# Bias of the first units as one fp32 pass, two modulation pieces in an earlier loop, and norm steps inside the mixers' order

## The reference

```
for l in range(DEPTH):                      # DEPTH = 2
    ml = adaln_chunks(sc_lat @ w_mod[l] + b_mod[l])      # 9 vectors of 1024: shift, scale, gate, three times
    mc = adaln_chunks(sc_ctx @ w_mod[l] + b_mod[l])
    xl = xl + 0.5 * ml[2] * swiglu(modulate(rms_norm(xl, norm_ffn1[l]), ml[0], ml[1]), ffn1_w13[l], ffn1_w2[l])
    xc = ...                                             # the same for the context tokens
    h_ctx = modulate(rms_norm(xc, norm_mix[l]), mc[3], mc[4])
    h_lat = modulate(rms_norm(xl, norm_mix[l]), ml[3], ml[4])
    mix_c, mix_l = hybrid_mixer(h_ctx, h_lat, ...)       # w_in, attention A, attention B, Mamba-2 scan
    xl = xl + ml[5] * (mix_l @ w_out[l])
    xl = xl + 0.5 * ml[8] * swiglu(modulate(rms_norm(xl, norm_ffn2[l]), ml[6], ml[7]), ffn2_w13[l], ffn2_w2[l])
def modulate(h, shift, scale): return h * (1 + scale) + shift
```

## Time and profile before

| what | value |
|---|---|
| median of three runs | 1889.11 us (1888.89 to 1890.87) |
| profiled execution, its own time | 1888.78 us |
| its span | 1887.1 us |
| TensorE busy | 1811.9 us (96%) |
| VectorE busy | 1423.3 us (75%) |
| ScalarE busy | 752.0 us (40%) |
| HBM read | 252.60 MB |
| TensorE on the chain that ended last | 84% |

### The profile page before, as it was taken

The page is one execution under the profiler, slowest core; times in us unless marked ns, Lnnn a source line. Parts: engine busy times, 40 slices in busy tenths (PEclk is TensorE's granted clock), DMA queues, the critical chain, the costliest instruction groups (busy, mean ns, idle before and its releaser), DMA issues.

```text
span 1887.1 us, 26111 instructions
## 1 busy us (share of the span) xinstructions
PE 1811.9 (96%) x9314; PEld 1496.1 (79%) x9314; DVE 1423.3 (75%) x2351; ACT 752.0 (40%) x1147; POOL 51.6 (3%) x101
## 2 busy tenths in 40 slices
PE   8999999997999899899999999999999799899999
PEld 5788888886776577688888888888888578589999
DVE  5887877788877767887777678777786888756665
ACT  4322222246656656222222372222224654754342
POOL 1000000000000000000000000000000000000000
PEclk8899999998998899899999999999999899979999
DMA  8444444422312033534444423444440332134543
GB/s 352 179 151 183 147 159 168 182 80 93 119 45 90 1 134 116 197 133 178 155 156 161 151 75 148 159 168 162 156 156 29 114 111 88 48 112 178 180 178 110
DMA packets 37585, 259.47 MB, mean 137 GB/s; under 512 B 4369, under 2 KB 5841, under 8 KB 7441
## 3 DMA queue, kind: packets, MB, share of 16 engines
q1 hardware_dynamic: 26066, 182.32, 26.5%
q0 software_dynamic: 11456, 76.32, 11.0%
HBM read 252.60 MB, written 5.24 MB: 137 GB/s over the span
## 4 chain that ended last, share of the span: by engine, by line
PE 84%; DVE 6%; ACT 6%; issue 3%; DMA 1%; POOL 0%; ACTq 0%; DVEq 0%; POOLq 0%
PE ps L1514 25%; PE ps L1515 25%; PE ps L1516 25%; PE ps L1622 1%; DVE mod_prod L951 1%; ACT w_hi L546 1%; ACT n_t L598 1%; PE ps L1830 1%; DMA scale_w<-scale_in 1%; PE ps L1772 1%; PE ps L1891 1%; PE ps L1795 1%; DVE x_res L1056 1%; PE ps L1805 1%; PE ps L1645 1%
## 5 line engine op out<-in xcount | busy, mean ns | idle before, releaser
L1514 PE MATMUL ps<-h_hi,w_hi 128*128 128x512 f32 (+1 forms) x1840 | 680.3, 370 | 26.3 <-DVE w_lo L933 10.4
L1515 PE MATMUL ps<-h_lo,w_hi 128*128 128x512 f32 (+1 forms) x1840 | 673.7, 366 | 0.0
L1516 PE MATMUL ps<-h_hi,w_lo 128*128 128x512 f32 (+1 forms) x1840 | 672.9, 366 | 0.0
L1514 PEld LDWEIGHTS ps<-h_hi,w_hi 128*128 128x128 f32 x1840 | 350.5, 190 | 90.7 <-issue 22.9
L1516 PEld LDWEIGHTS ps<-h_hi,w_lo 128*128 128x128 f32 x1840 | 350.2, 190 | 57.4
L1515 PEld LDWEIGHTS ps<-h_lo,w_hi 128*128 128x128 f32 x1840 | 350.6, 191 | 56.6 <-issue 1.2
L928 DVE TENSOR_TENSOR w_lo<-raw,w_hi 128x2048 fp32r<-128x2048 f32 x132 | 301.9, 2287 | 82.3 <-ACT w_hi L546 82.2
L1056 DVE SCALAR_TENSOR_TENSOR x_res<-ps,abg,x_res 128x256 f32<-128x256 f32 x584 | 248.4, 477 | 151.2 <-PE ps L1516 150.2
L546 ACT ACTIVATE w_hi<-raw 128x2048 fp32r<-128x2048 f32 x132 | 252.2, 1911 | 268.0 <-PE ps L1516 268.0
L951 DVE CUSTOM_DVE_ANT_0 mod_prod<-mod_raw,cb 128x1024 f32<-128x1024 f32 x256 | 301.5, 1218 | 2.6 <-ACT cb L738 2.5
L1514 PE MATMUL ps<-a_hi,w_hi 128*128 128x512 f32 (+1 forms) x640 | 235.5, 368 | 16.1 <-DVE x_res L1056 12.5
(11 more groups left out here) (231 smaller groups left out, 1594.9 us busy)
## 6 DMA issues: line engine op xcount, KB each, us to landing
raw<-ffn_in SPq DMA_DIRECT2D x132, 1024.0 KB, 4.8
mod_raw<-mod_in POOLq DMA_DIRECT2D x68, 1024.0 KB, 5.0
raw<-proj_in SPq DMA_DIRECT2D x20, 1024.0 KB, 4.9
raw<-out_w_in SPq DMA_DIRECT2D x8, 1024.0 KB, 4.7
x_spill<-x_res SPq DMA_DIRECT2D x2, 2048.0 KB, 7.2
x_res<-x_spill SPq DMA_DIRECT2D x2, 2048.0 KB, 7.9
scale_w<-scale_in POOLq DMA_DIRECT2D x4, 512.0 KB, 13.1
x_res<-x_in SPq DMA_DIRECT2D x2, 1024.0 KB, 11.3
```

Source lines behind the costliest of these rows:

```text
L1514: pe.matmul(dst, w_hi[:, slot, wsl], hi, start=first, stop=False)
L1515: pe.matmul(dst, w_hi[:, slot, wsl], lo, start=False, stop=False)
L1516: return pe.matmul(dst, w_lo[:, slot, wsl], hi, start=False, stop=last)
```

## The change

- **Bias.** `unit_bias` multiplies the fp32 weights in `raw` with the fp32 shift in `abg`, 16 matmuls of two columns in place of 32 fp32r ones of four. It stands at the start of `first_unit`, which also waits until PSUM bank 4 has been read. `shift_r`, its split on VectorE and the reduction go. Because `raw` slot 0 is read later, SP waits for `bias_mm` ahead of the FFN's loop of loads and ahead of a mixer's load 2. With 256 tokens the mean moves from k = 2 to k = 5.
- **Modulation pieces 14 and 15** leave the start of FFN 1. FFN 0's turns 1 to 4 take six tiles each (pieces 4 to 9), turns 5 to 9 four (10 to 14), the last turn piece 15.
- **Norm steps in the order.** In a mixer n.0 to n.8, e.0 (`first_scaled`), dv.0 (`derive`), la.0 (the layer's small vectors) and S.-1 (the split of unit 2) are steps of `WEAVE`; before, they were done ahead of all others. R is in five parts, and both lists are new throughout.

```
-        MOD_PRE = {0: (2, 2), 1: (14, 2)}
-        STRETCH = {0: [(1, PAIRS - 1, 4)], 1: [(1, PAIRS - 1, 16)], ...
-        LAST_PIECE = {0: 13}
+        MOD_PRE = {0: (2, 2)}
+        STRETCH = {0: [(1, 5, 4), (5, PAIRS - 1, 10)], 1: [(1, PAIRS - 1, 16)], ...
+        LAST_PIECE = {0: 15}
...
-                "cv.0 E.0 E.1 S.0 T0.0 T.2 E.2 R.0 R.1 R.2 E.3 cv.1 T.3 T.4 cv.2 S.1 R.3 E.4 E.5 si.0 cv.3 S.2 si.1 si.2 si.3 "
+                "dv.0 n.0 n.1 n.2 n.3 T0.0 T.2 Ta.4 n.4 n.5 e.0 la.0 S.-1 E.0 E.1 Tb.4 Ta.5 n.6 n.7 Tb.5 n.8 cv.0 E.2 R.0 R.1 E.3 "
...
-                "cv.0 T0.0 cv.1 T.2 E.0 E.1 E.2 R.0 R.1 T.3 T.4 T.5 S.0 E.3 si.0 T.6 T.7 E.4 R.2 S.1 cv.2 cv.3 R.3 S.2 E.5 E.6 "
+                "dv.0 la.0 T0.0 n.0 n.1 n.2 T.2 n.3 n.4 n.5 Ta.4 n.6 n.7 Tb.4 e.0 Ta.5 Tb.5 n.8 S.-1 cv.0 cv.1 E.0 E.1 E.2 Ta.6 "
...
                     sp.dma_start(raw_of(1), ffn_in[f, 1]).then_inc(raw_in[1], 16)
+
+                    sp.wait_ge(bias_mm, NORM_OF_FFN[f])
...
+                    if m == 2:
+                        sp.wait_ge(bias_mm, 3 * layer + 1)
...
-            def split_shift(n):
...
-                dve.tensor_reduce(bias[:, :, :], ps[:, BIAS_AT, 0:8]...
+                dve.tensor_copy(bias[:, :, :], ps[:, BIAS_AT, 0:4].rearrange("p (m s) -> p m s", m=2)).then_inc(bias_done, 1)
...
-                if f == 1:
-                    mod_pieces(q0, cnt // 2)
                 split(0, f, 1)
...
+                if f == 1:
+                    dve.wait_ge(cb_ready, 6)
...
-                turn(i, None if q is None else i + (q - lo))
+                    if (f, lo) == (0, 1):
+                        with dve.Fori(0, 2) as t:
+                            a, b, c = (tiles_of(3 * t + (q + k)) for k in range(3))
+                            turn(2 * t + 1, a + b[:2])
+                            turn(2 * t + 2, b[2:] + c)
...
-            def unit_bias(n, slot):
-                pe.wait_ge(shift_done, 2 * n)
+            def unit_bias(n):
+                pe.wait_ge(derive_s, DERIVED_AB[n])
                 for m in range(2):
                     for k in range(KT):
-                        ...two matmuls, w_hi and w_lo by shift_r[:, k, :]
+                        last = pe.matmul(ps[:, BIAS_AT, 2 * m:2 * m + 2], raw[:, 0, 256 * k + P * m:256 * k + P * m + P],
+                                         abg[:, n, 1, :, k], start=(k == 0), stop=(k == KT - 1))
...
                 split_ready(0, turn)
+                pe.wait_ge(*evac)
+                unit_bias(n)
                 for k in range(KT):
...
-                    if k == 2:
+                    if k == (2 if nt == T else 5):
                         mean(n, nt)
-                    elif k == 5:
-                        unit_bias(n, 0)
```

More of the change, by code:

```diff
@@ L480, in load_stretches @@
                 for lo, hi, q0 in STRETCH[f]:
-                    if q0 is not None:
+                    if (f, lo) == (0, 1):
+                        with pool.Fori(0, 2) as t:
+                            for q in range(3):
+                                load_piece(3 * t + (q0 + q))
+                    elif q0 is not None:
                         with pool.Fori(lo, hi) as i:
@@ L693, in mixer @@
                     if kind == "E":
-                        if j >= 2:
+                        if j < 2:
+                            first_evacuation(layer, j)
+                        else:
                             evacuate(layer, j)
+                    elif kind == "n" and j < KT:
+                        norm_tile(3 * layer + 1, j, T, base)
                     elif kind == "S":
@@ L743, in first_evacuation @@
                 act.wait_ge(pads, layer + 1)
-                for j in range(2):
-                    act.wait_ge(scaled_s, 2 * n - 1 + j)
-                    for s in range(2):
-                        x = act.activation(xpad[:, j, s, 2:2 + LAT], ps[:, j, s * LAT:(s + 1) * LAT], ACT.Identity, bias=bias[:, j, s:s + 1])
-                    x.then_inc(pj_evac, 1)
+                act.wait_ge(scaled_s, 2 * n - 1 + j)
+                for s in range(2):
+                    x = act.activation(xpad[:, j, s, 2:2 + LAT], ps[:, j, s * LAT:(s + 1) * LAT], ACT.Identity, bias=bias[:, j, s:s + 1])
+                x.then_inc(pj_evac, 1)
             def evacuate(layer, g):
@@ L870, in decay_rows @@
                     act.activation(lam[0:16, 72:76], r[2].rearrange("p (c t) -> p c t", c=TT)[:, :, P - 1], ACT.Exp).then_inc(row_act, 1)
-                else:
+                elif part == 4:
                     act.wait_ge(row_act, ra + 8)
@@ L1020, in first_scaled, with norm_tile @@
                     tt(ps[:, m, 0:nt], ps[:, m, 0:nt], n_rstd[:, 0:nt], ALU.mult).then_inc(scaled_s, 1)
[L1022 to L1031 removed]
+            def norm_tile(n, d, nt):
+                if d == 0:
+                    dve.wait_ge(acc_done, 7 * n + 7)
+                    dve.wait_ge(rstd_done, 2 * n + 2)
+                if d < KT:
                     if d >= 2:
@@ L1034, in norm_rest @@
                     tt(n_t[:, d % 2, 0:nt], x_res[:, d, 0:nt], n_rstd[:, 0:nt], ALU.mult).then_inc(t_done, 1)
-                    if d >= 1:
-                        remainder(d - 1)
+                if d >= 1:
+                    dve.wait_ge(h_hi_s, 8 * n + d)
+                    tt(h_lo[:, d - 1, 0:nt], n_t[:, (d - 1) % 2, 0:nt], h_hi[:, d - 1, 0:nt], ALU.subtract).then_inc(h_lo_s, 1)
+            def norm_rest(n, nt, after={}):
+                for d in range(KT + 1):
+                    norm_tile(n, d, nt)
                     if d in after:
                         after[d]()
-                remainder(KT - 1)
             def product(f, i, nt, hi, lo):
@@ L1087, in ffn_phase, with down @@
                 derive(n, "g")
-                def down(i, units, add_n=None, piece=None, gate_split=None):
+                if f == 1:
+                    dve.wait_ge(cb_ready, 6)
+                def down(i, units, add_n=None, tiles=(), gate_split=None):
                     for d in range(KT):
@@ L1099, in down @@
                             split(*gate_split)
-                        if piece is not None and d in (3, 7):
-                            mod_tile(piece, d // 4)
+                        if tiles and d in (3, 7):
+                            mod_tile(*tiles[d // 4])
                         if add_n is not None and d >= 2:
@@ L1105, in down, with turn @@
                             scaled_low(add_n[0], d - 1, add_n[1], h_hi, h_lo)
-                def turn(i, piece):
-                    down(i - 1, base + 3 * i + 1, piece=piece, gate_split=(2, f, i))
+                def turn(i, tiles):
+                    middle = 1 + len(tiles) // 2
+                    down(i - 1, base + 3 * i + 1, tiles=tiles[:2], gate_split=(2, f, i))
                     split(0, f, i + 1)
-                    if piece is not None:
-                        mod_tile(piece, 2)
+                    for tile in tiles[2:middle]:
+                        mod_tile(*tile)
                     dve.wait_ge(unit_done, base + 3 * i + 2)
@@ L1114, in turn, with tiles_of @@
                     split(1, f, i + 1)
-                    if piece is not None:
-                        mod_tile(piece, 3)
+                    for tile in tiles[middle:]:
+                        mod_tile(*tile)
+                def tiles_of(piece):
+                    return [] if piece is None else [(piece, j) for j in range(4)]
                 def last_turn(piece):
```

126 lines of the change are left out of this document (57 added, 69 removed), and 65 rows, old and new, of the table WEAVE.

## The result

| | before | changed |
|---|---|---|
| median | 1889.14 us (1888.89 to 1890.87, 4 runs) | 1901.12 us (1899.74 to 1902.55, 4 runs) |
| span of the profiled execution | 1887.1 us | 1900.7 us |

The ratio is 1.0061, with a 95% interval of 1.0044 to 1.0079: the change makes the kernel 12 us slower. The forecast was 1884.1 us, with a range that ended at 1895.

What follows compares the result with a forecast made beforehand. TensorE was taken as the bound, busy 1811.9 of 1887.1 us, with its waits and low clock as the loss. From 1888.78 us, -15.3 + 11.4 + 1.5 + 3.7 - 1 - 5 = -4.7 gave 1884.1 us, range 1874 to 1895.

Steps and rivals of the forecast that it cites:

- Pieces leave FFN 1: Start of FFN 1: two TensorE gaps (10.2 us) and the low clocks behind them (5.1 us) go, together -15.3 us.
- FFN 0's turns hide them: FFN 0: VectorE's added tiles fit into its idle time within some tenths of a microsecond, 0.
- The bias itself: All five entries: 16 fp32 matmuls take 3.5 us, as the 32 fp32r ones did, so 0.
- the rival of four passes: Bias in five entries: true fp32 takes four passes, 17.5 us more, 1901.6 us; chance 0.02.
- The late mean in the FFNs: FFN 1 and FFN 2 entries: TensorE waits 3.5 and 3.7 us for the activation, low clocks 2.1 us each, +11.4 us.
- Mixer 0 +1.5, mixer 1 +3.7 us: Mixer entries: the split of unit 2 and some tiles come later in the new order, costing 1.5 and 3.7 us.
- The replay: Mixer entries stepped through with the profile rows' durations; in mixer 0 it gave waits of 4.3 and 5 us.
- Attention -5 us: Attention in the mixers: the new order removes one gap and part of another, -5 us.
- SP's new waits, 0: SP's waits for the bias: loads behind it are needed 20 us later, so 0.
- FFN 3, -1 us: FFN 3's entry: bias fills the 2.51 us before the mean, mean 3 to 5 us later, net -1 us.
- The rival of the norm chain as the bound: Five entries: the mean behind the bias makes the norm chain the bound, 1893.7 or 1900.5 us; chance 0.20.

Runs made afterwards that it cites:

- the pieces alone: Kernel before with only modulation pieces 14 and 15 moved out of FFN 1 into FFN 0's turns, bias and lists as before: 1872.39 us, 1872.87 us when run again.
- old_lists: Changed kernel with each engine's order in the mixers as before, bias still ahead of the first unit: 1899.41 us, ratio 1.0056 to the kernel before.
- mean_second_old: Changed kernel with the old mixer lists and the mean directly behind the bias, ahead of the first unit's matmuls: 1876.32 us, ratio 0.9925 to the kernel before.
- bias_k5: Changed kernel with the fp32 bias moved back behind the sixth tile in the four entries of 512 tokens: 1881.34 us, ratio 0.9942 to the kernel before.
- hold_load: Kernel before with the pieces moved, fp32r bias and old lists, plus only SP's wait for the bias ahead of each mixer's load of unit 2: 1887.08 us.
- mean_second: Changed kernel with the mean directly behind the bias, ahead of the first unit's matmuls, in all five entries: 1872.93 us, ratio 0.9909 to the kernel before.
- mean_k4: Kernel before with the pieces moved and the mean two tiles later in entries of 512 tokens, bias untouched: 1882.71 us, ratio 0.9968 to the kernel before.

## Why the prediction was wrong

Point by point, by its own steps:

- *Pieces leave FFN 1, -15.3 us; FFN 0's turns hide them, 0.* Right: -15.4 us by itself, and FFN 0's turns unchanged. The profile of the whole program was 1.7 us late at mixer 0, but the pieces alone start it at 415.8 in one run and 417.6 in the other, so this is spread.
- *The bias itself, 0; the rival of four passes.* Right in the form: in FFN 1 both take 3.49 us, and two kernels that differ in the form alone have the same FFN 1 and FFN 2. The rule of the Trainium skill (FP8 and Floating Point Precision, Matmul Precision) that true fp32 takes four passes is not borne out as time here, for two columns: two records and 0.109 us each. But I had read the 3.5 us in mixer 0 alone. The kernel before already had 3.76 us in FFN 2, 3.70 in mixer 1 and 6.68 in FFN 3, at granted clocks of 0.92, 0.94 and 0.50.
- *The late mean in the FFNs, +11.4 us.* Right in mechanism, and 4.1 + 7.3 = 11.4 us; that the sum fits to a tenth is luck, since the parts (5.6 and 5.8) were off by 1.5 us each way. The mean is 5.2 us late in FFN 1 and 6.8 in FFN 2. TensorE waits 2.4 us in both; in FFN 2 alone low clock follows the wait (8 matmuls), and 13 follow the bias there where 5 did.
- *Mixer 0 +1.5, mixer 1 +3.7 us.* **This is the first step that failed.** The replay had the right waits in the right places (4.3 and 5 us in mixer 0), but with r 4.9 us late instead of 6.8, and with no low clock: every duration in it was taken at full speed. I had priced the clock behind the waits of the FFNs and left it out for the mixers, though the earlier trace rows stood before me with 8.63 us and 10.39 us of idle TensorE, and the seven half-clock matmuls behind the bias were in my own count. The 1.9 us by which the mean is later than forecast are themselves mostly clock: 0.75 us in the bias, and four more half-clock matmuls behind it. Behind the mean, 20 more rows in each entry of the changed trace are at half clock, 4 us. Put into the terms, mixer 0 becomes 1.5 + 1.9 + 4 = 7.4 us, against 7.2 measured; mixer 1 becomes 3.7 + 1.9 + 4 = 9.6, against 8.3, so there the replay's order had been too dear. The replay had also credited the new order with hiding lateness; old_lists has the same late mean, the old order, and entries of 68.2 and 68.4 us against 69.0 and 69.3, so it hid none.
- *Attention -5 us.* **The second step that failed**, by 5.3 us: in the changed kernel the stretches behind the entries are 0.2 us shorter and 0.5 us longer than before, and the two kernels with new lists and the mean on time show no gain in sum either. I named one gap that the order removes and did not look for where it opens others; where one of 3.31 us was, there are two of 3.5.
- *SP's new waits, 0.* Right for the changed kernel, where the bias is first. But the reason I gave, that the loads are needed 20 us later, was no reason: it holds because the bias stands first, with the old lists too (in mean_second_old ScalarE has no wait for the load of unit 2). With the bias at its old place ScalarE waits 1.8 us in mixer 0 if the split is late (bias_k5), and with the split at its old place too the wait costs 7 us per mixer (hold_load). I had not asked why the bias had been moved to the front.
- *FFN 3, -1 us.* +0.5 us. The mean is 7.1 us late there, not 3 to 5, and brought forward in mean_second it gave 5.7 us back; but +0.5 itself is within what its clock varies: with the same FFN 3 the kernel before took 210.8 us and the pieces alone 207.8.

The rival of the norm chain as the bound, to which I gave 0.20, is what happened. Its upper price, 4.9 us and 2.1 us of clock in each of four entries and nothing from attention, was 28 us and 1900.5 us; measured are 26.9 us in those four stages and 1901.1. The sum of the stages, -15.4 + 11.4 + 7.2 + 8.3 + 0.5 and 1.7 of spread, is the 13.6 us between the spans.

How much of the mixers' loss is lateness and how much clock is not separable in full: a later r opens and moves gaps, and the long ones in the mixers' entries were followed by low clock. In mean_k4, where the mean alone is 2.7 us late, the two entries are some 3 us longer each, but TensorE's idle time in them is as before (9.5 us against 9.8, 12.8 against 12.6) and the clock is lower (0.87 against 0.92). So that run doesn't separate them either.
